# The last layer's index scores stand between the two halves of the output projection, and the output rows are scaled after the scores

## The chip, the core and the metric

The kernel runs on one core of a Trainium2 chip. The metric is the device time of one execution in microseconds (us). Five engines work side by side, each on its own queue of instructions in program order: TensorE (PE in the profile, its weight loads PEld), VectorE (DVE), ScalarE (ACT), GpSimd (POOL) and the sync engine (SP), which here only issues DMAs. They wait for one another through semaphores. SBUF is the on-chip memory for operands, PSUM the eight banks that TensorE writes to. A difference in time counts as measured here if it is over 0.2%, 8.8 us.

## The reference

Five layers follow one another on 2048 rows of 1024 numbers. The change is in the last one, a sparse attention beside a linear one. For a query block of 128 rows the reference does this (cut to what matters):

```python
rel = einsum('bqhd,bsd->bqhs', iqb, ik)                      # 8 index heads of 64
score = einsum('bqh,bqhs->bqs', iwb, relu(rel))              # weighted sum over the heads
score = where(key_pos <= t, score, -inf)
_, sel = lax.top_k(score, 256)                               # the keys that this block attends to
logits = einsum('bqhr,bqkr->bqhk', qb, kv_sel) * 128**-0.5 + bias
p = softmax(logits); o = einsum('bqhk,bqkr->bqhr', p, kv_sel) # 4 heads, then w_uv and silu(z)
mix = concatenate([o_a, o_b], -1) @ w_out[layer]             # the output projection
x = x + gate * rmsnorm(mix, g_post)                          # scaled output rows, added to x
```

## The kernel before

The last layer (sparse_layer) starts at about 3100 us of the span. It has 16 blocks of 128 query rows, numbered 0 to 15. Each engine has its own program for it, a loop over the blocks i written out by hand; the order of the code is the order on the engine. Work is staggered: in block i the attention of block i runs, together with the search for the 256 best keys of block i+1 and the projections and index scores of block i+2.

A block begins with the logits of head 0 (TensorE, L2232), which VectorE scales and masks from PSUM (L2600), adds the position bias to (L2604, both inputs in SBUF) and takes the maximum of (L2605). ScalarE makes the exponentials (L2405). Meanwhile TensorE makes the first three tiles of the projection for block i+2 (L2179, 24 matmuls), and then, once the exponentials are there, transposes them (L2242). The other heads follow; VectorE and ScalarE take turns at the search in between. After the heads VectorE chooses the keys of block i+1. TensorE counts, over the partitions, the rows where the choice is not exact (L2329), VectorE reads the count (L2579, L2582) and takes a branch only if it is not zero: equal_scores (L2497 to L2503), seven operations over the whole width, which this document calls the tie branch. L2633 ends that step in either case.

The change is at the end of the block. TensorE's program has:

- mix_half(0): half of the output projection, eight matmuls of 128x512 into bank 6 (L2303)
- the count (L2329)
- mix_half(1): the other half, into bank 7
- score: the index scores of block i+2, into banks 2, 3, 5 and 4 in turn (L2321). There are 8 heads by up to 4 pieces of up to 512 keys, so 8, 16, 24 or 32 scores in blocks 0 to 13 and none in 14 and 15. The inputs are 64 deep; two heads lie in the two halves of the array and their matmuls run as a pair. Each pair from the third on waits for the relu of two pairs earlier

ScalarE squares and sums the two banks 6 and 7 (L2446), adds the sums and makes 1/rms (L2449 to L2453), then takes the relu of each score into one of four buffers (L2441, function rectify). VectorE multiplies banks 6 and 7 by 1/rms and the gate (L2653), then weighs and adds each relu into the score row (L2643 for the first head of a piece, L2646 for the others, function weigh), which frees a relu buffer. GpSimd adds x to the scaled rows (L2676) and, in the next block, multiplies z by its gate (L2672). SP stores the rows and loads the next ones when GpSimd is done.

A matmul with 32-bit inputs appears as two records, so eight matmuls of a half are x16.

Of the kernel before, what the change touches and what calls it, by code (L numbers as in the profile page):

```python
# [1988 lines left out]
def score_order(i):  # L1989


    pieces, order = key_chunks(i), []
    for first in range(0, len(pieces), 2):
        pair = pieces[first:first + 2]
        for turn in range(len(pair)):
            order += [(pair[(h + turn) % len(pair)], h) for h in range(IDX_HEADS)]
    return order
# [12 lines left out]
def sparse_layer(nc, x, g_kv, w_uv, rel_bias, w_out, consts, gate_row, hT_in, oa_in, bias_scratch, out,  # L2010
# [6 lines left out]
    with ExitStack() as ctx:  # L2017
# [80 lines left out]
        idx_made, relu_ready, relu_used = (Varied(sem(n), scored) for n in ("idx_made", "relu", "relu_used"))  # L2098
# [55 lines left out]
        def _(pe):  # L2154
# [57 lines left out]
            for i in range(BLOCKS):  # L2212
# [86 lines left out]
                def mix_half(half, first, last):  # L2299
                    for k in range(first, last):  # L2300
                        if not half:
                            pe.wait_ge(*catT_ready.upto(i, 1 + k // 4))
                        m = pe.matmul(bank[6 + half][:], catT[:, k * P:(k + 1) * P],  # L2303
                                      W_out[:, k, half * 512:(half + 1) * 512], start=(k == 0), stop=(k == KT - 1))
                    if (half, last) == (1, KT):
                        m.then_inc(*y_made.inc())

                def score(first, last):
                    for n in range(first, last, 2):
                        if n >= 4:  # L2310

                            pe.wait_ge(*relu_ready.upto(i + 2, n - 2))
                        elif n == 2:

                            pe.wait_ge(*cT_ready.upto(i + 2))
                            if FIRST_TOPK <= i + 1:
                                pe.wait_ge(*nbad_ready.upto(i + 1))
                        for m in (n, n + 1):
                            (a, w), h = score_order(i + 2)[m]
                            o = 64 * (h % 2)  # L2320
                            pe.matmul(bank[IDX_BANKS[m % 4]][:, 0:w], iqT[o:o + 64, h // 2, :], ikT[o:o + 64, a:a + w],  # L2321
                                      start=True, stop=True).then_inc(*idx_made.inc())
# [7 lines left out]
                scores = scored[i + 2] if i + 2 < BLOCKS else 0  # L2330
                if scores:
                    pe.wait_ge(*proj_ready.upto(i + 2, 2))
                mix_half(1, 0, KT)
                score(0, scores)

        @block.scalar
        def _(act):
# [54 lines left out]
            for i in range(BLOCKS):  # L2392
# [41 lines left out]
                def rectify(numbers):  # L2434

                    for n in numbers:
                        w = score_order(i + 2)[n][0][1]
                        act.wait_ge(*idx_made.upto(i + 2, n + 1))
                        if n >= 4:
                            act.wait_ge(*relu_used.upto(i + 2, n - 3))  # L2440
                        act.activation(relu[:, n % 4, 0:w], bank[IDX_BANKS[n % 4]][:, 0:w], ACT.Relu).then_inc(*relu_ready.inc())  # L2441

                scores = scored[i + 2] if i + 2 < BLOCKS else 0
                act.wait_ge(*y_made.upto(i))
                for half in range(2):
                    act.activation(squares[:, half * 512:(half + 1) * 512], bank[6 + half][:], ACT.Square,  # L2446
# [4 lines left out]
                act.activation(mrs[:], mss[:, 0:1], ACT.Ln, bias=eps[:, 0:1], scale=1.0 / D).then_inc(*o.inc())  # L2451
                o.settle()
                act.activation(mrs[:], mrs[:], ACT.Exp, scale=-0.5).then_inc(*mrs_ready.inc())  # L2453
                rectify(range(scores))
                o.end_block()

        @block.vector
        def _(dve):
# [130 lines left out]
            for i in range(BLOCKS):  # L2589
# [45 lines left out]
                def weigh(numbers):  # L2635
                    order = score_order(i + 2)
                    for n in numbers:
                        (a, w), h = order[n]
                        dve.wait_ge(*relu_ready.upto(i + 2, n + 1))
                        dst, weight = acc[:, a:a + w], iw[:, h:h + 1]  # L2640
                        earlier = [m for m in range(n) if order[m][0] == (a, w)]
                        if not earlier:
                            dve.tensor_scalar(dst, relu[:, n % 4, 0:w], weight, None, ALU.mult).then_inc(*relu_used.inc())  # L2643
                        else:
                            dve.wait_ge(*relu_used.upto(i + 2, earlier[-1] + 1))
                            dve.scalar_tensor_tensor(dst, relu[:, n % 4, 0:w], weight, dst, ALU.mult, ALU.add)\  # L2646
                               .then_inc(*relu_used.inc())

                scores = scored[i + 2] if i + 2 < BLOCKS else 0
                dve.wait_ge(*mrs_ready.upto(i))  # L2650
                for half in range(2):
                    sl = slice(half * 512, (half + 1) * 512)
                    dve.scalar_tensor_tensor(cat[:, sl], bank[6 + half][:], mrs[:, 0:1], gate_row[:, sl], ALU.mult, ALU.mult)\  # L2653
                       .then_inc(*(mix_ready if half else o).inc())
                weigh(range(scores))
                if scores:
                    dve.wait_ge(*relu_used.upto(i + 2))
                o.end_block()

        @block.gpsimd  # L2660
# [139 lines left out]
```

## Time and profile before

| | |
|---|---|
| median of 3 runs | 4403.19 us (4403.06 to 4405.84) |
| the profiled execution, whole | 4403.81 us |
| its span in the trace | 4402.0 us |
| mean granted TensorE clock | 0.969 of full speed |
| TensorE busy | 4045.2 us (92%) |
| VectorE busy | 1987.7 us (45%) |
| ScalarE busy | 1397.0 us (32%) |
| GpSimd busy | 780.2 us (18%) |

The profiled execution lies 0.6 us above the median of the runs. Busy time is a mean over five layers. A granted clock of 1.00 is 2.4 GHz, 0.50 is 1.2 GHz. Times in the rows are us from the start of the span. A row of the timeline may stand for several instructions of one kind; then its duration runs from the start of the first to the end of the last.

### The profile page before, as it was taken

To read this page: it belongs to the slowest core of one execution; us is meant where nothing else is said; L and a number is where in the kernel's file an instruction comes from. 1 tells how busy PE (TensorE), PEld (TensorE's weight loads), DVE (VectorE), ACT (ScalarE), POOL (GpSimd) and SP (SyncE) were. 2 spreads that over 40 slices of the span, in tenths; PEclk is the share of its full clock that TensorE was granted. 3 is DMA by queue.
4 is the path that set the end of the run, shared out by engine and by line. 5 is a ranking of instruction groups with operands and counts; after the bars stand their busy time and mean duration, and the time that the engine had idled before them with its cause. 6 is when DMAs were issued, how large, how long until landed. Compare 5 with 4: busy or idle time off the path is not lost. (4 is left out here: it accounts for less than half of the span.)

```text
span 4402.0 us, 57334 instructions
## 1 busy us (share of the span) xinstructions
PE 4045.2 (92%) x22955; PEld 2615.1 (59%) x22955; DVE 1987.7 (45%) x4350; ACT 1397.0 (32%) x2958; POOL 780.2 (18%) x544
## 2 busy tenths in 40 slices
PE   8999999998899999997999999996999989898877
PEld 4555555554455555544888888885666565565544
DVE  0111111111333333333456655553157676888875
ACT  2222222222111111111333333331245454555552
POOL 1323323323012222221122222221000000000000
PEclk9999999998999999998999999995999999999998
DMA  5000000002201111114000000002100000000000
GB/s 185 20 19 10 19 14 14 19 14 110 90 30 35 35 35 35 35 35 149 20 26 25 21 25 25 21 23 84 64 22 30 34 18 22 29 18 17 17 13 17
DMA packets 89739, 162.43 MB, mean 37 GB/s; under 512 B 17381, under 2 KB 49466, under 8 KB 89402
## 3 DMA queue, kind: packets, MB, share of 16 engines
q1 hardware_dynamic: 89530, 159.53, 10.6%
q8 instruction: 145, 2.38, 0.2%
q14 instruction: 64, 0.52, 0.0%
HBM read 120.18 MB, written 39.33 MB: 36 GB/s over the span
## 5 line engine op out<-in xcount | busy, mean ns | idle before, releaser
L349 PE MATMUL e_ps<-arena,e_xT 128*128 128x440 f32 (+1 forms) x1792 | 688.6, 538 | 2.7 <-DMA arena<-l_w_in 2.7
L863 PE MATMUL o_ps<-arena,o_xT 128*128 128x512 f32 x1280 | 564.5, 594 | 0.8 <-ACT o_xT L971 0.8
L349 PEld LDWEIGHTS e_ps<-arena,e_xT 128*128 128x128 f32 x1792 | 333.2, 191 | 304.1 <-issue 296.1
L863 PEld LDWEIGHTS o_ps<-arena,o_xT 128*128 128x128 f32 x1280 | 239.3, 191 | 279.1 <-issue 279.0
L1393 PE MATMUL d_ps<-hT_in,arena 128*128 128x128 f32 x3072 | 392.2, 282 | 13.4 <-ACT hT_in L1579 11.4
L1393 PEld LDWEIGHTS d_ps<-hT_in,arena 128*128 128x128 f32 x3072 | 359.4, 193 | 29.0 <-ACT hT_in L1579 12.6
L2179 PE MATMUL s_ps<-hT_in,arena 128*128 128x128 f32 x2160 | 257.6, 280 | 7.0 <-PEq L67 7.0
L2179 PEld LDWEIGHTS s_ps<-hT_in,arena 128*128 128x128 f32 x2160 | 254.1, 197 | 10.9 <-issue 9.9
L952 PE MATMUL o_ps<-o_w_out,o_gt 128*128 128x512 f32 x512 | 225.3, 598 | 4.6 <-ACT o_gt L1028 4.6
L2303 PE MATMUL s_ps<-arena 128*128 128x512 f32 x512 | 227.1, 597 | 0.0
L2321 PE MATMUL s_ps<-s_ikT,s_iqT 64*128 64x512 f32 (+3 forms) x608 | 170.3, 640 | 61.6 <-ACT s_Lg L2441 60.8
L446 PE MATMUL e_ps<-e_w_out,e_gt 128*128 128x512 f32 x512 | 224.1, 596 | 0.0
L475 ACT ACTIVATE e_hh<-e_ps 128x440 f32<-128x440 f32 (+1 forms) x112 | 60.3, 538 | 451.5 <-PE e_ps L349 451.5
L622 DVE SCALAR_TENSOR_TENSOR e_gl<-xb,e_ps 128x512 f32<-128x512 f32 x32 | 20.6, 684 | 397.5 <-PE e_ps L446 397.5
L1780 DVE SCALAR_TENSOR_TENSOR d_cT<-d_cv,d_convw,d_cT 128x128 f32<-128x128 f32 x576 | 186.3, 397 | 1.2
L2250 PE MATMUL s_ps<-s_pT,s_ckvr 128*128 128x128 f32 x1088 | 154.0, 284 | 26.7 <-ACT s_pT L2418 26.2
L2441 ACT ACTIVATE s_Lg<-s_ps 128x512 f32<-128x512 f32 (+3 forms) x304 | 153.1, 543 | 70.2 <-DVE s_acc L2643 31.6
L2646 DVE SCALAR_TENSOR_TENSOR s_acc<-s_Lg,s_iw,s_acc 128x512 f32<-128x512 f32 (+3 forms) x266 | 171.3, 700 | 8.9 <-ACT s_Lg L2441 2.8
L952 PEld LDWEIGHTS o_ps<-o_w_out,o_gt 128*128 128x128 f32 x512 | 96.6, 191 | 123.8 <-issue 116.2
L2250 PEld LDWEIGHTS s_ps<-s_pT,s_ckvr 128*128 128x128 f32 x1088 | 136.8, 195 | 52.9 <-ACT s_pT L2418 49.0
L2545 DVE TENSOR_SCALAR_CACHE_REDUCE s_passed<-s_acc,s_mid 128x384 bf16<-128x384 f32 (+13 forms) x112 | 165.7, 1480 | 4.0
L446 PEld LDWEIGHTS e_ps<-e_w_out,e_gt 128*128 128x128 f32 x512 | 96.8, 192 | 115.9 <-issue 115.9
(416 smaller groups left out, 6161.1 us busy)
## 6 DMA issues: line engine op xcount, KB each, us to landing
xb<-x SPq DMA_DIRECT2D x64, 512.0 KB, 3.4
o_scratch<-w_ada SPq DMA_DIRECT2D x16, 768.0 KB
arena<-l_w_in SPq DMA_DIRECT2D x5, 2048.0 KB, 19.6
arena<-w_in SPq DMA_DIRECT2D x5, 2048.0 KB, 13.4
x<-e_gl SPq DMA_DIRECT2D x16, 512.0 KB
x<-o_cat SPq DMA_DIRECT2D x16, 512.0 KB
hT<-hT_in SPq DMA_DIRECT2D x16, 512.0 KB, 2.6
out<-xb SPq DMA_DIRECT2D x16, 512.0 KB, 2.9
```

Of the source, the lines that this page charges most:

```text
L349: m = pe.matmul(bank[c % 2][:, 0:n], xT[:, k * P:(k + 1) * P], W_in[:, k, a:a + n], start=(k == 0), stop=(k == KT - 1))
L446: m = pe.matmul((zk, bTp)[half][:], catT[:, k * P:(k + 1) * P], W_out[:, k, half * 512:(half + 1) * 512], start=(k == 0), stop=(k == KT - 1))
L863: m = pe.matmul(bank[c % 2][:], xT[:, k * P:(k + 1) * P], W_in[:, k, off:off + 512], start=(k == 0), stop=(k == KT - 1))
L952: m = pe.matmul((y0, y1)[half][:], catT[:, k * P:(k + 1) * P], W_out[:, k, half * 512:(half + 1) * 512], start=(n == 0), stop=(n == KT - 1))
L1393: m = pe.matmul(bank[c % 2][:, t * P:(t + 1) * P], W_in[:, k, (4 * c + t) * P:(4 * c + t + 1) * P], hT[:, k * P:(k + 1) * P], start=(k == ...
L1780: m = dve.scalar_tensor_tensor(cT[:, t, :], cv[:, p, t, j:j + P], convw[:, j, t:t + 1], cT[:, t, :], ALU.mult, ALU.add)
L2179: m = pe.matmul(out_[:, t * P:(t + 1) * P], W_in[:, k, tile_of(c, t)], source[:, k * P:(k + 1) * P], start=(k == 0), stop=(k == KT - 1))
L2250: m = pe.matmul(bank[5][:, h * P:(h + 1) * P], ckvr[:, a // P + t, :], pT[:, n % 4, t, :], start=(c == 0 and t == 0), stop=(a + (t + 1) * ...
L2303: m = pe.matmul(bank[6 + half][:], catT[:, k * P:(k + 1) * P], W_out[:, k, half * 512:(half + 1) * 512], start=(k == 0), stop=(k == KT - 1))
L2321: pe.matmul(bank[IDX_BANKS[m % 4]][:, 0:w], iqT[o:o + 64, h // 2, :], ikT[o:o + 64, a:a + w], start=True, stop=True).then_inc(*idx_made.inc())
L2545: do(dve.tensor_scalar(passed[:, 0:W], acc[:, 0:W], mid[:, 0:1], 0.0, ALU.is_ge, ALU.add, accum_out=cnt[:]))
L2646: dve.scalar_tensor_tensor(dst, relu[:, n % 4, 0:w], weight, dst, ALU.mult, ALU.add)\
```

## The change

For each block, TensorE issues the scores after the first half and the count, and the second half after the scores. ScalarE takes all relus of the block before the squares of the projection, and VectorE weighs all scores before it scales the output rows. The work itself is the same: no instruction is added or taken away. The second half and its statistics now follow up to 32 scores, and what comes of them (GpSimd's addition, the store, the next load on SP) follows too.

```diff
@@ tensor, end of a block
                 scores = scored[i + 2] if i + 2 < BLOCKS else 0
                 if scores:
                     pe.wait_ge(*proj_ready.upto(i + 2, 2))
+                score(0, scores)
                 mix_half(1, 0, KT)
-                score(0, scores)
@@ scalar, end of a block
                 scores = scored[i + 2] if i + 2 < BLOCKS else 0
+                rectify(range(scores))
+
                 act.wait_ge(*y_made.upto(i))
                 for half in range(2):
                     act.activation(squares[:, half * 512:(half + 1) * 512], bank[6 + half][:], ACT.Square,
...
                 act.activation(mrs[:], mrs[:], ACT.Exp, scale=-0.5).then_inc(*mrs_ready.inc())
-                rectify(range(scores))
                 o.end_block()
@@ vector, end of a block
                 scores = scored[i + 2] if i + 2 < BLOCKS else 0
+                weigh(range(scores))
+                if scores:
+                    dve.wait_ge(*relu_used.upto(i + 2))
+
                 dve.wait_ge(*mrs_ready.upto(i))
                 for half in range(2):
                     sl = slice(half * 512, (half + 1) * 512)
                     dve.scalar_tensor_tensor(cat[:, sl], bank[6 + half][:], mrs[:, 0:1], gate_row[:, sl], ALU.mult, ALU.mult)\
                        .then_inc(*(mix_ready if half else o).inc())
-                weigh(range(scores))
-                if scores:
-                    dve.wait_ge(*relu_used.upto(i + 2))
                 o.end_block()
```

TensorE at the end of block 9, whose 24 scores all have one shape, as the difference between the two programs (s_ps are the PSUM banks; s_bad the count's input; s_ikT, s_iqT the index keys and queries):

```order
 L2303 MATMUL s_ps<-arena 128x512 x8
 L2329 MATMUL s_ps<-s_bad,s_ones 1x2
-L2303 MATMUL s_ps<-arena 128x512 x8
 L2321 MATMUL s_ps<-s_ikT,s_iqT 128x512 x24
+L2303 MATMUL s_ps<-arena 128x512 x8
 L2232 MATMUL s_ps<-s_ckvT,s_qbT 128x512 x2
 L2232 MATMUL s_ps<-s_ckvT,s_qbT 128x384
```

The second half has moved behind the 24 scores and stands directly ahead of the next block's logits (L2232).

VectorE at the same place, the program before (xb holds the scaled rows, s_Lg the relu buffers and the logits, s_acc the score row):

```order
L2633 COPY s_lo<-s_ones 128x1
L2653 SCALAR_TENSOR_TENSOR xb<-s_ps,s_mrs,gate_row 128x512 x2
L2643 TENSOR_SCALAR s_acc<-s_Lg,s_iw 128x512 x2
L2646 SCALAR_TENSOR_TENSOR s_acc<-s_Lg,s_iw,s_acc 128x512 x14
L2643 TENSOR_SCALAR s_acc<-s_Lg,s_iw 128x512
L2646 SCALAR_TENSOR_TENSOR s_acc<-s_Lg,s_iw,s_acc 128x512 x7
L86 ISA
L2600 SCALAR_TENSOR_TENSOR s_Lg<-s_ps,s_selb 128x512 x2
```

And the changed program (its lines are numbered one to five higher here):

```order
L2634 COPY s_lo<-s_ones 128x1
L2644 TENSOR_SCALAR s_acc<-s_Lg,s_iw 128x512 x2
L2647 SCALAR_TENSOR_TENSOR s_acc<-s_Lg,s_iw,s_acc 128x512 x14
L2644 TENSOR_SCALAR s_acc<-s_Lg,s_iw 128x512
L2647 SCALAR_TENSOR_TENSOR s_acc<-s_Lg,s_iw,s_acc 128x512 x7
L2658 SCALAR_TENSOR_TENSOR xb<-s_ps,s_mrs,gate_row 128x512 x2
L86 ISA
L2601 SCALAR_TENSOR_TENSOR s_Lg<-s_ps,s_selb 128x512 x2
```

The scaling of the output rows stood ahead of the 24 weighings and now stands behind them, directly ahead of the next block's logits (L2600 before, L2601 after).

## Rows read from the trace of the kernel before

**Rows 1.** The page, costliest groups: count, busy us and mean ns, idle before.

```profile
L2303 PE MATMUL s_ps<-arena 128*128 128x512 f32 x512 | 227.1, 597 | 0.0
```

**Rows 2.** What the scaling L2653 waited for in all: us, times.

```profile
  ACT s_mrs L2453: 88.7, 11
```

**Rows 3.** Timeline, end of block 10: start, us, engine, line, operands, [idle <-releaser].

```profile
3906.74 7.13 PE L2303 MATMUL s_ps<-arena 128*128 128x512 f32 x16
...
3908.75 0.15 DVE L2633 COPY s_lo<-s_ones 128x1 f32<-128x1 f32 x1 [1.68 <-issue]
...
3916.10 1.41 DVE L2653 SCALAR_TENSOR_TENSOR xb<-s_ps,s_mrs,gate_row 128x512 f32<-128x512 f32 x2 [7.20 <-ACT s_mrs L2453]
...
3917.09 2.11 PE L2321 MATMUL s_ps<-s_ikT,s_iqT 64*128 64x512 f32 x8 [1.30 <-ACT s_Lg L2441]
3917.43 2.97 DVE L2643 TENSOR_SCALAR s_acc<-s_Lg,s_iw 128x512 f32<-128x512 f32 x2
3917.59 2.52 POOL L2676 TENSOR_TENSOR xb<-xb 128x1024 f32<-128x1024 f32 x1 [37.46 <-DVE xb L2653]
...
3920.32 9.55 DVE L2646 SCALAR_TENSOR_TENSOR s_acc<-s_Lg,s_iw,s_acc 128x512 f32<-128x512 f32 x14
...
3930.28 4.92 PE L2321 MATMUL s_ps<-s_ikT,s_iqT 64*128 64x512 f32 x20 [0.20 <-ACT s_Lg L2441]
...
3937.26 1.89 DVE L2600 SCALAR_TENSOR_TENSOR s_Lg<-s_ps,s_selb 128x512 f32<-128x512 f32 x3
...
3939.18 0.43 DVE L2604 TENSOR_TENSOR s_Lg<-s_Lg,s_bias 128x256 f32<-128x256 f32 x1
```

**Rows 4.** Timeline, end of block 11.

```profile
4007.65 0.20 ACT L2453 ACTIVATE s_mrs<-s_mrs 128x1 f32<-128x1 f32 x1
...
4012.47 0.15 DVE L2633 COPY s_lo<-s_ones 128x1 f32<-128x1 f32 x1 [0.34 <-DVE s_selb L2503]
...
4013.86 2.96 DVE L2643 TENSOR_SCALAR s_acc<-s_Lg,s_iw 128x512 f32<-128x512 f32 x2
...
4024.21 8.09 PE L2321 MATMUL s_ps<-s_ikT,s_iqT 64*128 64x512 f32 x32 [0.27 <-ACT s_Lg L2441]
...
4034.86 2.08 DVE L2600 SCALAR_TENSOR_TENSOR s_Lg<-s_ps,s_selb 128x512 f32<-128x512 f32 x4
```

**Rows 5.** Timeline, start of block 3.

```profile
3311.49 6.27 PE L2179 MATMUL s_ps<-hT_in,arena 128*128 128x128 f32 x48
...
3311.73 0.69 DVE L2600 SCALAR_TENSOR_TENSOR s_Lg<-s_ps,s_selb 128x512 f32<-128x512 f32 x1 [0.62 <-PE s_ps L2232]
3312.25 1.27 POOL L2672 TENSOR_TENSOR s_z<-s_z,arena 128x512 f32<-128x512 f32 x1 [10.13 <-ACT arena L2402]
3312.46 1.33 DVE L2604 TENSOR_TENSOR s_Lg<-s_Lg,s_bias 128x256 f32<-128x256 f32 x1
...
3314.55 0.72 ACT L2405 ACTIVATE s_Lg<-s_Lg,s_mx 128x512 f32<-128x512 f32 x1 [2.38 <-DVE s_mx L2605]
...
3317.59 0.60 PE L2242 MATMUL s_ps<-ident,s_Lg 128*128 128x128 f32 x4
```

**Rows 6.** Timeline of GpSimd and VectorE in layer two.

```profile
1209.07 2.46 POOL L1186 TENSOR_TENSOR o_cat<-o_cat,o_ln_grow 128x1024 f32<-128x1024 f32 x1 [43.24 <-DVE o_cat L1147]
1209.24 2.57 DVE L1090 TENSOR_TENSOR o_rc<-o_qk,arena 128x256 f32<-128x256 f32 x1
...
1211.61 2.42 POOL L1188 TENSOR_TENSOR o_cat<-o_cat,o_ln_brow 128x1024 f32<-128x1024 f32 x1
```

**Rows 7.** Windows of TensorE: stretch, us, PE busy (records), granted clock, DMA share, GB/s.

```profile
3303.00:3313.00 10.00, 10.00 (x26) 0.50 0.38 129
...
4011.00:4016.20 5.20, 0.00 (x0) 1.00 0.00 0
4016.20:4023.00 6.80, 5.45 (x14) 0.50 0.57 195
4023.00:4032.00 9.00, 8.73 (x38) 1.00 0.00 1
```

## The prediction

> **What bounds the kernel now.** I read the page first, then the timeline of the ends of two blocks of the last layer, then what the scaling of the output rows waits for, then the windows with the granted clock. The page says that TensorE is nearly always busy, and that the halves of the output projection (L2303) cost 227 us with no wait before them [rows 1]. That is a mean over five layers; the change touches fourteen places of some 30 us each, the ends of blocks 0 to 13 of the last layer, so those have to be read singly.
>
> The end of block 10 shows the order in time [rows 3]. VectorE has chosen its keys at 3908.90. TensorE runs the second half of the projection until 3913.87, ScalarE then makes the squares and 1/rms until 3916.10, VectorE scales two rows of 512 (1.41 us), and only at 3917.43 does it start to weigh. Its two first weighings take 2.97 us, though two of them back to back elsewhere take 0.87 (0.48 each, a little overlapped): the second ends 0.3 us after GpSimd's 2.52 us addition. From there VectorE is the pace, one 512-wide weighing each 0.66 us (14 in 9.55), with TensorE and ScalarE waiting for free buffers. The last score ends at 3935.20, the next block's first logits (L2600) start at 3937.26. VectorE's wait for 1/rms is 88.7 us in all, over 11 of 16 blocks [rows 2].
>
> Block 11 is of the other kind [rows 4]: equal scores make VectorE take the branch that breaks ties, so it is free only at 4012.62, after 1/rms was long ready (4007.85). In blocks 2, 3, 5, 6, 11 and 12 the branch is taken; in 0, 1, 4, 7, 8, 9, 10 and 13 it is not. This split decides the sum.
>
> **First part: where the second half goes.** After the change, the last score's end E is followed by the second half, 16 records at 0.43 us, 6.9; the statistics, 3916.10 - 3913.87 = 2.2; and the scaling, 1.4 [rows 3]. So the next logits start at E + 10.5. VectorE's own last weighing ends only 1.4 to 5.5 us after E, so it then waits 5 to 8 us: a new wait in place of the old one.
>
> In a block without a tie E comes earlier by two amounts: the weighing starts at 3908.9 instead of 3917.43, 8.5, and GpSimd's addition has moved behind it, 2.1. Together 10.6. The gain is then (time from E to the next logits before) + 10.6 - 10.5. For block 10: 2.1 + 0.1 = 2.2 us. The same rows read in blocks 4, 7, 8, 9 and 13 give 2.4, 3.4, 4.1, 5.8 and 3.9; six blocks, 21.8 us. I take off 2 us, since before the weighing starts with four sums' inputs ready and afterwards it starts on an empty pipe. Blocks 0 and 1 have eight scores, which never meet a full buffer: four pairs of about 1 us (two pairs took 2.11) [rows 3] from the end of the first half, then 10.5, give 3.7 and 5.4. Sum of the eight: 29 us gained.
>
> In a tie block VectorE is late anyway. Block 11: the weighing starts 4013.86 - 4012.62 = 1.2 earlier and loses the 2.1 stall, 3.3; from E to the next logits it was 4034.86 - 4032.30 = 2.6. So 2.6 + 3.3 - 10.5 = -4.6. TensorE did the second half inside the tie branch at no cost, and now does it in the open. Blocks 2, 3, 5, 6 and 12 give -2.6, -3.4, -3.2, -4.6 and -4.0. Sum of the six: 22.4 us lost. Net of this part: 6.7 us gained.
>
> **Second part: GpSimd's addition.** It now starts with the next block's logits, and the waiting multiplication of z (1.27 us) follows it. The trace shows which VectorE instructions suffer: L2600 reads PSUM and keeps its 0.69 us beside the multiplication, L2604, with both inputs in SBUF, takes 1.33 us in place of 0.43 [rows 3, 5]. So L2604 will end about 0.25 us after the addition, 2.9 us after the first logits started. Before it ended 1.0 to 2.8 us after (1.25 in block 1, growing with the keys). The delays over the fourteen next blocks add up to 12.7 us, 1.7 and 1.9 in the first two, 0.4 or less in the last three. Does the multiplication slip in ahead of the waiting L2604? In layer two a VectorE operation that waits between two GpSimd ones ends 0.28 us after the first of them [rows 6]; so I take no.
>
> Not all of the 12.7 reaches TensorE. At the start of block 3 TensorE was in the projection (L2179, 6.27 us, done at 3317.76) long after the exponentials (3315.27) [rows 5]. After the change the projection starts before the logits are read, and the exponentials release the transposes at +4.65 instead of +5.86. Counted at the first transpose, blocks 3, 4 and 7 gain 1.2, 1.7 and 0.6, the other eleven lose 9.5 (block 2 the most, 1.9): 6.1 us lost. Bounds: 0, if TensorE's other waits cover it, and 12.7, if VectorE's search is the chain everywhere; with the multiplication ahead, another 1.0 x 13. The row nearest is the first transpose's, so 6.1.
>
> **Third part: the clock.** TensorE had nothing between 4011.0 and 4016.2 in block 11, and its granted clock fell to 0.50, the 1.2 GHz level, for the next 6.8 us [rows 7]; in block 2 it stood at 0.50 for 10 us of scores. After the change the gap in tie blocks is longer: after the first half and eight scores (3.5 us) TensorE is idle until VectorE comes, about 4 us in blocks 2 and 3, 6 in 5 and 6, 11 in 11 and 12. Then come the scores that are left, and behind them the second half. Where the low stretch reaches into that half, each 3.4 us of it costs 1.7. I charge 1 us to blocks 2, 3 and 5, which have least work between the gap and the second half, and nothing to the others: 3 us. Bounds: 2 us gained, as short low stretches in blocks 4, 7, 9 and 13 should vanish with the gap that caused them; 18 us lost, if each tie block has 6 us more of the low clock in work that cannot wait (half of it is the cost, 3).
>
> The Trainium skill has a rule that speaks against this change: TensorE: Matmul & The Clock Gate, section "HAM oscillation — how this bites in real kernels", says in effect that an array which idles between bursts begins each burst at the lower rate and pays the transition every time. The trace agrees for the gap of block 11. If every tie block paid it in the second half too, the sum would be the slower rival's below.
>
> **What else moves.** ScalarE's three operations for the gate of z now follow 1/rms, and are done before the exponentials need ScalarE. The output rows leave some 20 us later; the store, the load of the other layer's rows and of x follow on SP's queue, and have the 30 to 60 us of the next block before their first use. TensorE's wait for the scaled rows, before the next block's first transposes, stands behind an exponential that comes later. All at nothing. The last two blocks have no scores and stay as they are.
>
> **Sum.** 4403.8 (the profiled execution, 0.6 above the median) - 6.7 + 6.1 + 3 = 4406.2, say 4406: no change that could be measured.
>
> **Rivals.** (1) The clock. The second half runs at 1.2 GHz in tie blocks. For it: the gaps double, and block 2 already shows 10 us of scores at the low level. Against: blocks 11 and 12 have some 15 us of scores between the gap and the half, and the clock was back before that (1.00 from 4023.0). Six blocks x 3 us = 18 in place of 3: 4421. It counts as slower once it takes over 10 us in all, 1.7 per tie block. (2) L2604 meets both GpSimd operations or its delay runs through VectorE's chain: 12.7 + up to 13 in place of 6.1, 4413 to 4426. Rows 6 speak against the larger. (3) Faster: the delay of L2604 is hidden (0), the low stretches outside the ties vanish (2 gained in place of 3 lost), and ties cost 0.7 us less each, because the freed VectorE starts on eight ready scores (4): 4403.8 - 6.7 - 2 - 4 = 4391. For it: TensorE is what is busiest, and it loses idle time in eight blocks. Against: in six it gains more idle time per block.
>
> **Chances.** Forecast 0.56; rival 1 0.17; rival 2 0.11; rival 3 0.16. A measurement tells 0.2%, 8.8 us, from no change. Faster 0.16, same 0.57, slower 0.27. The range runs from rival 3 to the middle of the slower ones: 4391 to 4420.
>
> **What would show it.** After the change, in every block 0 to 13, a wait of 5 to 8 us of VectorE for 1/rms behind the weighing; the first two weighings back at 0.87 us; L2604 of about 2 us at the start of blocks 1 to 3, shrinking to 0.5 by block 12. Blocks without a tie must be 2 to 5 us shorter, tie blocks 3 to 5 longer. I am wrong if the tie blocks lose nothing, which would mean that TensorE's own queue was the limit there, or if the granted clock is 0.50 in the second half of most of them.

## The result, and the profile after

The changed kernel takes 4414.18 us at the median of 20 runs, the kernel before 4403.8 over 20 runs. One of the 20 took 7941.92 us at a granted clock of 0.871 and is left out of the ratio; without it the median is 4413.78. The ratio is 1.0023, with a 95% interval of 1.0017 to 1.0029: slower by 10 us, just beyond the 0.2% that I had set for a difference, though the interval begins just under it. The forecast was 4406, no change, with a range of 4391 to 4420. So the time lies in the range and the sign was not forecast. The profiled execution took 4415.49 us with a span of 4413.7, which is 11.7 more than before. Line numbers of the changed kernel are one to five higher: the scaling is L2658, the weighings L2644 and L2647, L2601 and L2605 are what L2600 and L2604 were, the addition is L2678. The page's row of the projection shows the first oddity, 609 ns for a record in place of 597 [rows 1]; 5.4 of the 5.9 us more lie in three second halves, those of blocks 2, 6 and 7:

```profile
L2303 PE MATMUL s_ps<-arena 128*128 128x512 f32 x512 | 233.0, 609 | 0.0
```

And what the scaling waits for (us, times) is 112.1 us over 15 blocks, where it was 88.7 over 11 [rows 2]:

```profile
  ACT s_mrs L2455: 112.1, 15
```

The end of block 10, which has no tie, in the timeline of the changed kernel (start, us, engine, line; the columns are those of [rows 3]):

```profile
3913.16 0.87 DVE L2644 TENSOR_SCALAR s_acc<-s_Lg,s_iw 128x512 f32<-128x512 f32 x2
...
3913.95 9.55 DVE L2647 SCALAR_TENSOR_TENSOR s_acc<-s_Lg,s_iw,s_acc 128x512 f32<-128x512 f32 x14
...
3928.77 7.13 PE L2303 MATMUL s_ps<-arena 128*128 128x512 f32 x16
...
3938.20 1.41 DVE L2658 SCALAR_TENSOR_TENSOR xb<-s_ps,s_mrs,gate_row 128x512 f32<-128x512 f32 x2 [7.45 <-ACT s_mrs L2455]
...
3939.52 1.88 DVE L2601 SCALAR_TENSOR_TENSOR s_Lg<-s_ps,s_selb 128x512 f32<-128x512 f32 x3
3939.69 2.36 POOL L2678 TENSOR_TENSOR xb<-xb 128x1024 f32<-128x1024 f32 x1 [55.22 <-DVE xb L2658]
3941.43 0.90 DVE L2605 TENSOR_TENSOR s_Lg<-s_Lg,s_bias 128x256 f32<-128x256 f32 x1
3942.01 1.45 POOL L2674 TENSOR_TENSOR s_z<-s_z,arena 128x512 f32<-128x512 f32 x1
```

The two first weighings take 0.87 us, not 2.97; they begin 2.1 us after the first half, not 10.7 us. The last score ends at 3928.84, the second half follows, the scaling waits 7.45 us, and the next logits start at 3939.52, 10.7 us after the last score. GpSimd's addition now begins 0.2 us after those logits, and L2605 lasts 0.90 in place of 0.43. The 10.7 us hold in eleven of the fourteen blocks; in 2, 6 and 7 it is 13.2, 12.4 and 11.9. The wait for 1/rms has not gone, it has changed places with the weighing: behind it VectorE waits 10.5 us in block 2 and 4.8 to 8.6 in the other thirteen.

The end of block 11, which has the tie branch, of the same kernel [rows 4]:

```profile
4004.74 2.11 PE L2321 MATMUL s_ps<-s_ikT,s_iqT 64*128 64x512 f32 x8 [0.31 <-ACT s_Lg L2441]
...
4016.46 0.87 DVE L2644 TENSOR_SCALAR s_acc<-s_Lg,s_iw 128x512 f32<-128x512 f32 x2
...
4018.17 4.39 PE L2321 MATMUL s_ps<-s_ikT,s_iqT 64*128 64x512 f32 x12 [11.32 <-ACT s_Lg L2441]
...
4032.43 7.13 PE L2303 MATMUL s_ps<-arena 128*128 128x512 f32 x16
...
4041.86 1.41 DVE L2658 SCALAR_TENSOR_TENSOR xb<-s_ps,s_mrs,gate_row 128x512 f32<-128x512 f32 x2 [6.80 <-ACT s_mrs L2455]
...
4043.19 2.08 DVE L2601 SCALAR_TENSOR_TENSOR s_Lg<-s_ps,s_selb 128x512 f32<-128x512 f32 x4
```

TensorE has done eight scores at 4006.85 and then waits 11.32 us for a relu buffer, since VectorE is in the tie branch until 4016.5. That is where the second half used to run. Now it runs at 4032.43, and everything waits for it.

The time from the start of the first half to the next block's first logits, before and after, is the measure of the block ends. All fourteen, in us, beside the forecast for each:

| block | 0 | 1 | 4 | 7 | 8 | 9 | 10 | 13 | sum |
|---|---|---|---|---|---|---|---|---|---|
| no tie, forecast | -3.7 | -5.4 | -2.4 | -3.4 | -4.1 | -5.8 | -2.2 | -3.9 | -29 (2 taken off) |
| measured | -3.8 | -5.1 | -3.2 | -1.7 | -3.6 | -5.7 | -2.1 | -3.8 | -28.9 |

| block | 2 | 3 | 5 | 6 | 11 | 12 | sum |
|---|---|---|---|---|---|---|---|
| tie, forecast | +2.6 | +3.4 | +3.2 | +4.6 | +4.6 | +4.0 | +22.4 |
| measured | +5.6 | +3.8 | +4.5 | +6.4 | +4.4 | +4.1 | +28.7 |

The block starts (next logits to the first transpose) are 4.3 us longer in the sum, the remainders of the blocks (first transpose to the next first half) 5.5 us. With 0.1 from the ends (block 14's, 0.3 longer, is in it) this is 9.95 us; another 1.7 of the 11.7 arise ahead of the first changed instruction, where the granted clock stood at 0.50 for 3.4 us more, and are no work of the change.

Block by block the remainders follow the clock. Behind the first transposes of blocks 3, 4, 9 and 11 there is a new stretch at 0.50, and these remainders are 1.6, 1.7, 1.3 and 1.2 us longer. Block 14 has 2.5 us more at 0.50 and is 2.4 longer. Blocks 1 and 2 had such stretches before and have none now; they are 1.6 and 2.7 us shorter.

Block 2 and the starts of blocks 3 and 5 in the same trace show why the tie blocks lost more than forecast, and what the remainders are:

```profile
3296.02 9.64 PE L2303 MATMUL s_ps<-arena 128*128 128x512 f32 x16
...
3306.36 5.52 PE L2179 MATMUL s_ps<-hT_in,arena 128*128 128x128 f32 x48
...
3307.96 1.41 DVE L2658 SCALAR_TENSOR_TENSOR xb<-s_ps,s_mrs,gate_row 128x512 f32<-128x512 f32 x2 [10.45 <-ACT s_mrs L2455]
...
3309.28 0.68 DVE L2601 SCALAR_TENSOR_TENSOR s_Lg<-s_ps,s_selb 128x512 f32<-128x512 f32 x1
3309.45 2.35 POOL L2678 TENSOR_TENSOR xb<-xb 128x1024 f32<-128x1024 f32 x1 [49.74 <-DVE xb L2658]
3310.00 2.08 DVE L2605 TENSOR_TENSOR s_Lg<-s_Lg,s_bias 128x256 f32<-128x256 f32 x1
...
3313.80 0.63 PE L2242 MATMUL s_ps<-ident,s_Lg 128*128 128x128 f32 x4 [1.92 <-ACT s_Lg L2405]
...
3452.78 0.63 PE L2242 MATMUL s_ps<-ident,s_Lg 128*128 128x128 f32 x4 [1.97 <-ACT s_Lg L2405]
```

The second half takes 9.64 us, in block 11 it took 7.13. The addition holds L2605 for 2.08 us, as [rows 5] suggested, and TensorE, whose projection ended at 3311.88, idles 1.92 us before the transposes. The granted clock (third number from the end in each row: us, PE busy, clock, DMA share, GB/s) of seven stretches of the same kernel: one in block 2, two in block 11, two in block 6, and the starts of blocks 3 and 5:

```profile
3287.50:3301.00 13.50, 12.11 (x22) 0.50 0.00 0
4012.00:4018.00 6.00, 0.00 (x0) 0.50 0.00 0
4022.00:4032.00 10.00, 9.25 (x40) 1.00 0.01 2
...
3591.50:3597.50 6.00, 3.90 (x27) 1.00 0.00 0
3598.10:3601.50 3.40, 3.40 (x5) 0.50 0.01 2
...
3314.00:3317.40 3.40, 3.40 (x16) 0.61 0.74 229
3452.80:3456.20 3.40, 3.40 (x23) 1.00 0.67 223
```

In block 2 the low clock, 1.2 GHz, lasts from the gap through the scores into the second half. In block 11 it begins in the gap and is over before the half. Block 6 is a third case: the stretch that began in its gap was over by 3591.5, the scores behind it ran at 1.00 with short waits (busy 3.90 of 6.00 us), and a second low stretch then fell into the half. Block 7, which has no tie and no such gap, has one too, and its half takes 8.35 us. At the start of block 3 a new low stretch begins behind the idle time. At the start of block 5 the idle time is as long, 1.97 us, and the clock stays at 1.00: eleven starts (blocks 1 to 11) have a gap of 1.9 to 2.1 us, and four of them are followed by a low stretch.

### The profile page after: what moved, and what is told of

Read it like the earlier page. It is cut to its first block and busy times, and to the rows that moved or that the text cites. A ratio compares the mean times of both kernels' runs of the same rounds, so it can differ in the third digit from the quotient of the medians.

```text
span 4413.7 us, 57334 instructions
## 1 busy us (share of the span) xinstructions
PE 4042.8 (92%) x22955; PEld 2616.3 (59%) x22955; DVE 1967.0 (45%) x4350; ACT 1395.1 (32%) x2958; POOL 779.8 (18%) x544
## 5 line engine op out<-in xcount | busy, mean ns | idle before, releaser
L2678 POOL TENSOR_TENSOR xb<-xb 128x1024 f32<-128x1024 f32 x16 | 37.7, 2356 | 884.1 <-DVE xb L2658 884.1
L2303 PEld LDWEIGHTS s_ps<-arena 128*128 128x128 f32 x512 | 97.3, 195 | 122.3 <-issue 121.7
L2647 DVE SCALAR_TENSOR_TENSOR s_acc<-s_Lg,s_iw,s_acc 128x512 f32<-128x512 f32 (+3 forms) x266 | 165.6, 679 | 9.4 <-ACT s_Lg L2441 3.3
```

## The experiments

**The order chosen by block.** TensorE's part of the edit; ScalarE's and VectorE's follow the same condition.

```diff
+TIED = (2, 3, 5, 6, 11, 12)
-                score(0, scores)
-                mix_half(1, 0, KT)
+                if i in TIED:
+                    mix_half(1, 0, KT)
+                    score(0, scores)
+                else:
+                    score(0, scores)
+                    mix_half(1, 0, KT)
```

> The changed order only in blocks 0, 1, 4, 7, 8, 9, 10 and 13, where no tie branch runs with these inputs; blocks 2, 3, 5, 6, 11 and 12 keep the order of the kernel before. Theory (the cost sits in the tie blocks, the gain in the others, and they are independent): in the trace of the changed kernel the eight blocks are together 21 us shorter than before (first half to next first half) and the six are 31 us longer, so this kernel takes 4403.8 - 21 = 4383 us, from 4378 to 4390. Rival (the change costs something in every block, say by the clock, that only shows in others): over 4395. Rival (an effect is handed on from a block without a tie to the tie block after it): the six blocks are then longer than before by over 1 us each, 4390 or more.

Measured: 4377.07 us, ratio 0.9943 (0.993 to 0.9956). The sign of each kind of block is what was claimed, and both rivals fall. It is 6 us better than the middle of the forecast and 1 us below its range: the ends of blocks 7 and 3 are 1.6 and 1.5 us shorter than the sums had them, where a low-clock stretch is missing. The new low stretches at block starts now lie in blocks 5 and 8, and not in 3, 4, 9 and 11. The blocks of either order are picked for these inputs; with others the ties lie elsewhere.

**VectorE's part alone.** In the kernel before, the scaling is moved behind the weighing, as in the diff of the change; TensorE and ScalarE stay.

```diff
-                dve.wait_ge(*mrs_ready.upto(i))
-                for half in range(2):
-                    sl = slice(half * 512, (half + 1) * 512)
-                    dve.scalar_tensor_tensor(cat[:, sl], bank[6 + half][:], mrs[:, 0:1], gate_row[:, sl], ALU.mult, ALU.mult)\
-                       .then_inc(*(mix_ready if half else o).inc())
                 weigh(range(scores))
                 if scores:
                     dve.wait_ge(*relu_used.upto(i + 2))
+                dve.wait_ge(*mrs_ready.upto(i))
+                for half in range(2):
+                    sl = slice(half * 512, (half + 1) * 512)
+                    dve.scalar_tensor_tensor(cat[:, sl], bank[6 + half][:], mrs[:, 0:1], gate_row[:, sl], ALU.mult, ALU.mult)\
+                       .then_inc(*(mix_ready if half else o).inc())
```

> The kernel before, with VectorE's part of the change alone: it weighs the scores first and scales the output rows last; TensorE and ScalarE keep their old order. Theory: the weighing starts 0.9 us earlier and loses the 2.1 us stall by GpSimd's addition, then the scaling costs 1.4 at the end, so 1.6 us are gained ahead of the next logits in each of 14 blocks, 22 us. The addition now holds up L2604 as it does in the changed kernel, which cost it 4.3 us at the first transposes and some 5 us in later low-clock stretches: 4403.8 - 22 + 10 = 4392, from 4386 to 4400. Rival (VectorE's stall is not on the path, TensorE is): 4403 or more. Rival (the delay of L2604 is what made the changed kernel slow): about 4410.

Measured: 4390.12 us, ratio 0.9972 (0.9962 to 0.9982), against 4392. So this part of the change is a gain of 13 us by itself, with the delay of L2604 in it; that delay is not enough to make the whole slower. That the time came out close is in part luck: the ends gained 28.6 us in place of 22 (those of blocks 2 and 3, 4.0 and 2.8, lost a low stretch), and the starts and remainders cost 14.7 in place of 10. The start of block 14 shows what the others avoid. In its timeline (VectorE's and GpSimd's rows) VectorE is not yet waiting with its addition of the bias when GpSimd is done with the first operation:

```profile
4223.44 2.35 POOL L2677 TENSOR_TENSOR xb<-xb 128x1024 f32<-128x1024 f32 x1 [62.40 <-DVE xb L2657]
...
4225.75 1.27 POOL L2673 TENSOR_TENSOR s_z<-s_z,arena 128x512 f32<-128x512 f32 x1
...
4226.29 1.00 DVE L2604 TENSOR_TENSOR s_Lg<-s_Lg,s_bias 128x256 f32<-128x256 f32 x1
```

GpSimd's next one starts at 4225.75, and L2604, which begins at 4226.29, lasts until it is over, 1.00 us. Where VectorE already waited, it came first, as in [rows 6] and at the start of the changed kernel's block 11: L2605 ended at 3942.33, 0.28 after the addition.

**The gap filled with spare work.** In the changed kernel:

```diff
-                score(0, scores)
+                score(0, min(scores, 8))
+                if i in TIED:
+                    for k in range(KT):
+                        pe.matmul(bank[7][:], catT[:, k * P:(k + 1) * P], W_out[:, k, 512:1024], start=(k == 0), stop=(k == KT - 1))
+                if scores > 8:
+                    score(8, scores)
                 mix_half(1, 0, KT)
```

> The changed kernel, with the second half's eight matmuls run once more into the same bank in the six tie blocks, after the first eight scores, where TensorE idles for 4 to 11 us; the values are written over later. Theory that the clock costs 5 us in the tie blocks (the second half takes 9.6 us in block 2 and 8.8 in block 6 at the low clock in place of 7.1): those come back to 7.1 and the low stretches before them vanish; in blocks 2 and 3 the spare work is longer than the gap and takes back 1 to 3 us. 4414.2 - 5 + 2 = 4411. Rival 1 of the prediction (the clock is most of the cost): 4400 or less. Rival (the clock is nothing): 4416 or more.

Measured: 4404.79 us, ratio to the kernel before 1.0008 (0.9999 to 1.0016). Forty-eight spare matmuls make the changed kernel 9.4 us faster by the medians, three times what I expected; by the two ratios, 1.0023 and 1.0008, it is some 6.6, since four of the twelve runs took 4409 to 4412 us. The time alone lies between my 4411 and rival 1's 4400 or less; the block ends have to decide. Block 2 in its timeline, TensorE: eight scores, the spare half, and further on the real one:

```profile
3279.78 3.96 PE L2322 MATMUL s_ps<-s_ikT,s_iqT 64*128 64x512 f32 x16
...
3283.67 7.13 PE L2337 MATMUL s_ps<-arena 128*128 128x512 f32 x16
...
3294.47 7.13 PE L2304 MATMUL s_ps<-arena 128*128 128x512 f32 x16
```

and the granted clock of two stretches in it, behind the spare half's start and in the real half:

```profile
3287.00:3291.00 4.00, 4.00 (x12) 1.00 0.00 0
3294.50:3301.50 7.00, 7.00 (x18) 1.00 0.00 0
```

The half of block 2 is back at 7.13 us; that of block 6 still takes 8.33, as its second low stretch is still there. In the traces the ends of blocks 2, 3, 5 and 6 are 3.2, 1.0, 1.1 and 0.2 us shorter, 5.4 in all, which is the expected part. In blocks 11 and 12 the low stretches are 6.8 us shorter each and nothing is gained. The other 4.6 come from places the spare work does not touch (the end of block 7, 1.6, that of block 14, 0.3, the remainders of block 14, 2.5, and of block 4, 1.2, less 1.0 in block 5). In the remainders and in block 7 a low stretch is gone or shorter, or is new in block 5; why they fell elsewhere is open. The 5.4 in the ties fit my 5 and not rival 1. I take 5.4 as the ties' share of the clock's cost in these traces, net of what the spare work itself takes.

**GpSimd's addition cut to eight columns,** in the changed kernel and in the kernel before, on one chip:

```diff
-                pool.tensor_tensor(xb[:], xb[:], cat[:], ALU.add).then_inc(*out_ready.inc())
+                pool.tensor_tensor(xb[:, 0:8], xb[:, 0:8], cat[:, 0:8], ALU.add).then_inc(*out_ready.inc())
```

> The changed kernel, with GpSimd's addition of x cut to 8 of 1024 columns (so 1016 columns of the output are not x plus the scaled rows but x alone). Theory: L2604 no longer waits 0.4 to 1.9 us, and is held only by the multiplication of z (1.27 us, up to 0.9 as before the change). The first transposes come 4 us earlier in the sum and the low-clock stretches at the starts of blocks 3, 4, 9 and 11, which cost some 5 us, vanish: 4414.2 - 9 = 4405, from 4402 to 4409. Rival (the delay is hidden, the loss is all in the six tie blocks): 4413 or more.

Measured: 4395.64 us, 18.5 under the changed kernel. I expected half of that. The start of block 3 in its timeline:

```profile
3305.41 0.68 DVE L2601 SCALAR_TENSOR_TENSOR s_Lg<-s_ps,s_selb 128x512 f32<-128x512 f32 x1
3305.57 0.20 POOL L2678 TENSOR_TENSOR xb<-xb 128x8 f32<-128x8 f32 x1 [49.35 <-DVE xb L2658]
...
3305.96 1.27 POOL L2674 TENSOR_TENSOR s_z<-s_z,arena 128x512 f32<-128x512 f32 x1 [0.18 <-ACT arena L2402]
3306.12 1.39 DVE L2605 TENSOR_TENSOR s_Lg<-s_Lg,s_bias 128x256 f32<-128x256 f32 x1
...
3309.22 0.63 PE L2242 MATMUL s_ps<-ident,s_Lg 128*128 128x128 f32 x4 [1.22 <-ACT s_Lg L2405]
```

L2605 is now held by the multiplication of z, 1.39 us, the transposes come 0.7 us earlier than after the change, and TensorE idles 1.22 us before them instead of 1.92. Summed over the blocks the first transposes come 9.1 us earlier; I had counted 4. And 6.9 us more fall away later in blocks 3, 4, 9, 11 and 14, where the low-clock stretch behind the transposes is gone or shorter. So the addition's cost at the starts is 16 us, of which the forecast had the delay itself and not the low clock that follows it. Only block 14's start has a gap over 1.7 us now, and no low stretch stands behind the transposes of any other block. Another 2.1 us are the last block's addition, at the very end of the kernel.

> The kernel before, with the same cut of the addition. Theory: the second weighing no longer waits 2.1 us, and as VectorE sets the pace of the scores, up to 14 x 2.1 = 29 us are gained, less where two head pieces of unlike width leave VectorE idle anyway (blocks 2, 3): 4378, from 4374 to 4386. Rival (the stall is covered, ScalarE and TensorE set the pace): 4400 or more.

Measured: 4364.01 us, ratio 0.9908 (0.9892 to 0.9925), 40 us gained. The two first weighings of block 10, with the cut addition beside them:

```profile
3886.61 0.88 DVE L2643 TENSOR_SCALAR s_acc<-s_Lg,s_iw 128x512 f32<-128x512 f32 x2
3886.77 0.37 POOL L2676 TENSOR_TENSOR xb<-xb 128x8 f32<-128x8 f32 x1 [37.46 <-DVE xb L2653]
```

0.88 us in place of 2.97. The block ends are 32.8 us shorter, 2.1 in most blocks as reckoned, 4.8 and 3.6 in blocks 2 and 3, which I had marked down and which lost a low stretch instead. The starts and remainders give 4.9 more and the end of the kernel 2.1, so the time lies 10 us below the range that I gave. A GpSimd operation of 2.5 us that seems to lie beside everything costs 40 us in 16 blocks. The two runs together say one more thing: with the thin addition the changed order is 31.6 us slower (4395.64 against 4364.01), since there is no stall left that it could take out of the weighing. About 30 us of what the change gains at the block ends are that stall.

**No tie branch,** in both kernels:

```diff
-                with dve.If(equal > 0):
+                with dve.If(equal > P):
                     equal_scores(W)
```

> The changed kernel, with the tie branch never taken (rows with equal scores at the threshold keep too many keys). Theory: all 14 blocks are then of the kind that gains; TensorE waits for nothing between the halves. Against the kernel before without the tie branch (the next run) it is 45 us faster at the block ends, less 10 for L2604 and the clock at the starts: 35 us faster. Rival (the cost is in the clock and in L2604, not in the ties): within 10 us of the next run, or slower.

> The kernel before, with the tie branch never taken. Theory: in blocks 2, 3 and 5 the branch ends before 1/rms is there, and costs nothing; in 6, 11 and 12 it holds up the scaling by 0.8, 4.8 and 5.6 us, and in block 14 by 7.2: 18 us less, 4385, from 4380 to 4392. Rival (the branch is on the path in full, some 10 us in each of 7 blocks): under 4350.

Measured: 4344.73 and 4389.94 us. The change, slower by 10 us with the ties, is faster by 45 without them. All fourteen block ends are shorter, by 51.8 us in the sum, and 7.3 come back at the starts and after. The 45 are 10 more than I expected. Block 11 of the changed kernel without the branch:

```profile
3965.89 0.15 DVE L2634 COPY s_lo<-s_ones 128x1 f32<-128x1 f32 x1 [1.52 <-issue]
...
3982.01 7.13 PE L2303 MATMUL s_ps<-arena 128*128 128x512 f32 x16
...
3991.43 1.41 DVE L2658 SCALAR_TENSOR_TENSOR xb<-s_ps,s_mrs,gate_row 128x512 f32<-128x512 f32 x2 [6.80 <-ACT s_mrs L2455]
...
3992.76 2.08 DVE L2601 SCALAR_TENSOR_TENSOR s_Lg<-s_ps,s_selb 128x512 f32<-128x512 f32 x4
```

VectorE is free 2.0 us after the first half's end and not 14. Removing the branch from the kernel before gains only 15 us: 0.7, 4.8, 5.4 and 7.1 at the ends of blocks 6, 11, 12 and 14, 18 in all as forecast, less 3.3 that come back behind them, and nothing in 2, 3 and 5, where the second half covered the branch. This is the strongest of the runs: the data decide the sign.

**Eight scores, the second half, the other scores.** TensorE's and ScalarE's part:

```diff
-                score(0, scores)
+                score(0, min(scores, 8))
                 mix_half(1, 0, KT)
+                score(8, scores)
...
-                rectify(range(scores))
+                rectify(range(min(scores, 8)))
                 act.wait_ge(*y_made.upto(i))
...
+                rectify(range(8, scores))
```

> A version between the two: first half, eight scores, second half, the other scores; ScalarE makes eight relus, then the statistics, then the other relus; VectorE weighs all and scales last. Theory: the second half is done in the tie branch again and the statistics lie beside the weighing, so nothing but the 1.4 us scaling stands at the end. With no tie and 16 or more scores: weighing 9 waits until 13.6 us after the first half, in place of 18 before, so 4.4 - 1.4 = 3 us gained; with a tie the stall of 2.1 is saved and the 1.4 at the end was there before: 2 us. Blocks 0 and 1 are as in the changed kernel, 9 us gained together. 9 + 6 x 3 + 6 x 2 = 39, less 10 for L2604 and its low-clock stretches: 4403.8 - 29 = 4375, from 4370 to 4388. Rival (any score order leaves the sum as it is, since TensorE is 92% busy): 4400 or more.

Measured: 4375.19 us, ratio 0.9939 (0.9926 to 0.9952), as forecast, and nearly so by its terms: 8.9, 14.8 and 14.3 us gained at the ends of blocks 0 and 1, of the six without a tie and of the six with one, for 9, 18 and 12, and 10.2 lost at the starts and after, for 10. Block 11 in its timeline:

```profile
3976.67 2.11 PE L2321 MATMUL s_ps<-s_ikT,s_iqT 64*128 64x512 f32 x8 [0.31 <-ACT s_Lg L2442]
...
3978.71 7.13 PE L2303 MATMUL s_ps<-arena 128*128 128x512 f32 x16
...
3988.39 0.87 DVE L2646 TENSOR_SCALAR s_acc<-s_Lg,s_iw 128x512 f32<-128x512 f32 x2
...
3990.09 3.44 PE L2321 MATMUL s_ps<-s_ikT,s_iqT 64*128 64x512 f32 x8 [4.25 <-ACT s_Lg L2442]
...
3993.11 0.20 ACT L2456 ACTIVATE s_mrs<-s_mrs 128x1 f32<-128x1 f32 x1
...
4009.01 2.37 POOL L2680 TENSOR_TENSOR xb<-xb 128x1024 f32<-128x1024 f32 x1 [62.09 <-DVE xb L2660]
```

The second half runs from 3978.71 to 3985.84, inside the tie branch; 1/rms is there at 3993.31, long before the weighing ends, and VectorE does not wait for it, here or in any of blocks 2 to 13. The last row is the addition, behind the next logits.

**The addition in two halves,** alone and on top of the two best orders. GpSimd's part; VectorE signals each half:

```diff
-                pool.wait_ge(*mix_ready.upto(i))
                 pool.wait_ge(x_in.sem, 16 * i + 16)
-                pool.tensor_tensor(xb[:], xb[:], cat[:], ALU.add).then_inc(*out_ready.inc())
+                for half in range(2):
+                    sl = slice(half * 512, (half + 1) * 512)
+                    pool.wait_ge(*mix_ready.upto(i, half + 1))
+                    pool.tensor_tensor(xb[:, sl], xb[:, sl], cat[:, sl], ALU.add).then_inc(*(out_ready if half else added).inc())
```

> The kernel before, with only GpSimd's addition in two halves. Theory (the second weighing waits for the end of the addition, whatever its parts): the addition starts 0.7 us earlier relative to the weighing, the stall of 2.1 shrinks to 1.4 in 14 blocks: 4403.5 - 9 = 4394, from 4390 to 4398. Rival (VectorE gets in between the two halves): the first weighing ends first and the stall is under 1.4, 4385. Rival (two additions cost GpSimd more than one): 4403 or more.

> The version with eight scores, the second half, the other scores in every block (4375.2 before), and GpSimd's addition in two halves as in the run beside it. It needs no knowledge of where ties fall. 4375.2 - 7 = 4368, from 4363 to 4374. Rival (covered): 4375.

> The order chosen by block, and GpSimd's addition in two halves. The six tie blocks have eight scores, the second half, the other scores; the other eight have the changed order. GpSimd adds the first 512 columns while VectorE still scales the second 512. From the blocks of the two orders as measured apart, the choice by block is 36 us faster than the kernel before: 4368. The halves end the addition 0.7 us earlier in 14 blocks, and where L2604 was held (blocks 1 to 10 as next blocks) that is 7 us and one or two low-clock stretches less; in blocks 11 to 13 the multiplication of z may now start before L2604 and hold it 0.6 longer: 4403.5 - 36 - 7 = 4360, from 4355 to 4368. Rival (the delay at the block starts is covered): 4368 or more.

Measured: 4393.86 (0.9977, 0.9968 to 0.9986), 4369.22 (0.9922, 0.9908 to 0.9935) and 4363.7 us (0.9901, 0.9886 to 0.9917). In the first, at the end of block 10:

```profile
3906.53 1.41 DVE L2654 SCALAR_TENSOR_TENSOR xb<-s_ps,s_mrs,gate_row 128x512 f32<-128x512 f32 x2 [7.20 <-ACT s_mrs L2454]
3907.43 2.67 POOL L2679 TENSOR_TENSOR xb<-xb 128x512 f32<-128x512 f32 x2 [36.87 <-DVE xb L2654]
...
3907.86 2.53 DVE L2644 TENSOR_SCALAR s_acc<-s_Lg,s_iw 128x512 f32<-128x512 f32 x2
```

The additions begin 0.9 us after the scaling does (1.5 before) and end 3.6 us after its start, in place of 4.0, and the two weighings take 2.53 in place of 2.97. That is 0.4 us a block, nearly 6 of the 10 us gained. The others lie where low stretches are shorter: the end of block 3 gains 1.5 more, the starts of blocks 3, 4 and 7 together 4.0, of which block 7 gives back 1.2 later, and the remainder of block 2 another 1.2. VectorE did get in between the two additions: its first weighing ended 0.28 us after the first addition, at 3908.98, and its second 0.29 after the second. It gained nothing by it, since the first weighing, which took 0.48 before, now waits too. In the last two kernels L2604 meets the multiplication of z at the starts of blocks 12 to 14, as the forecast for the last allowed: when it begins, just after the second addition, the multiplication is already under way, and it takes 1.2 to 1.5 us in place of 0.4. Both kernels beat the kernel before and the changed one; 4369.22 needs no list of blocks.

## Why the prediction was right, and where it was short

- The new wait (first part): right. The two kinds of block, their signs and their sizes came out within 1 us in ten of fourteen blocks. The forecast of E + 10.5 was 10.7 in eleven. That the gain of 29 came out as 28.9 is in part luck: six of the eight blocks without a tie fell short by 1.1 us together, which is what the 2 us for the empty pipe were for, and then block 4 gained 0.8 too much, its low stretch gone, and block 7 gained 1.7 too little, its half at the low clock.
- The stall by GpSimd's addition, 2.1 in the weighing and a delay of the bias addition afterwards: right. The delays add up to 11.0 us, 12.7 forecast, and the first transposes lost 4.3, 6.1 forecast. The guess that the multiplication of z does not go ahead while VectorE waits held at all fourteen starts of the changed kernel.
- The clock (third part): right in kind, too small. This is the term that was mis-sized: 3 us charged, for the tie blocks alone. By the run that filled the gap these paid 5.4, of which block 2's second half, 2.5 us longer, is the largest; block 6's half, 1.7 longer, was hit by a low stretch that did not come straight from its gap. The starts and remainders I had at nothing: new low stretches behind the transposes of four blocks took 5.8 us and block 14's 2.4, and the ones that went from blocks 1 and 2 gave back 4.3. I had looked at TensorE's gaps only inside the block ends. In block 3 the gap before the transposes grew from nothing to 1.9 us. The low stretches at the ends of blocks 4, 9 and 13 did vanish, as forecast; that of block 7 moved into its second half. Over the last layer the clock stood at 0.50 for 111 us before and for 125 after.
- What stays open is which gap is followed by a low stretch. Eleven starts have nearly the same gap and four pay; in the kernel ordered by block the same gaps paid at two other starts. Before the change block 10 had a gap of 3.2 us there and no low stretch. So the clock's share could be bounded beforehand and hardly be added up block by block.
- Rival 1 named the right term at too high a price, 18 us in the tie blocks for 5.4. The rule of the Trainium skill (TensorE: Matmul & The Clock Gate, "HAM oscillation — how this bites in real kernels"), that every burst behind an idle time begins at the lower rate, agrees with the traces in all six tie blocks: gaps of 4.2 to 12.1 us, and the clock at 0.50 when the scores went on. That every second half would pay does not follow, and they differ: the halves of 3, 5, 11 and 12 took 7.13 us, since the scores between the gap and the half had given the clock back.
- Rival 2's times, 4413 to 4426, hold the measured one, but its mechanism is not there: L2605 ended 0.28 us after the addition at every start and never met the multiplication, and the first transposes moved by 4.3 us and not 12.7. Rival 3 falls: the time is 23 us above its 4391.
- The sum: -6.7 + 6.1 + 3 = +2.4 forecast. Measured +10.4 at the median. The trace has 0.1 for the ends (-6.7 and the clock's 3 forecast), 4.3 for the starts (6.1) and 5.5 for the remainders (nothing); 1.7 of its difference lies ahead of the change. So the error is 3.8 us at the ends and 5.5 in the remainders, nearly all of it the clock's, less 1.8 at the transposes.
- Two readings were off and changed nothing: the 227 us of [rows 1] are of the last layer alone, whose 16 blocks have all 512 records, and the 10 us at 0.50 in block 2 [rows 7] were 7 us of scores and the beginning of the next block.

## What to carry to other kernels

Work that hides in another engine's slack is free only where that slack is: moving it gains or loses by block, and a branch that depends on the data can decide the sign, so count the blocks of each kind. When a wait is moved, look for what is late next and for the idle time it makes on TensorE, since a gap of 2 us can be followed by a stretch at the low clock, here in four of eleven places at 1.2 to 1.7 us each. Where no order is best for all blocks, split the work: eight scores ahead of the second half and the rest behind kept most of the gain in either kind of block, 28 us in all.

## What the runs showed of the hardware that I had not expected

- A 2.5 us GpSimd operation with both inputs in SBUF cost VectorE 1.9 to 2.1 us in each of 14 weighings, and up to 1.9 us at the block starts after it was moved there. Cutting it to eight columns gained 40 us in the kernel before and 18.5 in the changed one. Cutting it in two gained 10.
- Between two GpSimd operations the VectorE operation that already waited went first: it ended 0.28 us after the first of them, at all fourteen block starts of the changed kernel. One that began 0.5 us after the second had started took 1.00 us in place of 0.43.
- Spare matmuls in a gap made the kernel 9.4 us faster by the medians: the granted clock stood at 1.00 through the end of block 2, where it had been 0.50 for 13.5 us.
- The clock fell while TensorE was idle (0.50 from 4012 to 4018, with no matmul, in block 11 of the changed kernel) and was back at 1.00 from 4022 on, with scores running. In block 2 it stayed low from the gap until the second half was well under way. In the kernel before, the 5.2 us gap of block 11 passed at 1.00, and the low stretch came behind it [rows 7].
